# A decoder layer on one core: how the weights of merge, out and FFN are split into two parts

## The reference, cut to what matters

```python
g_a, g_b, g_m = jnp.split(sigmoid(g_raw + b_gate), N_BRANCH, axis=-1)
m = g_a * (o_mla @ w_o_mla) + g_b * (o_ssm @ w_o_ssm) + g_m * (o_mem @ w_o_mem)
x1 = layer_norm(ALPHA * x + m @ w_out, ln1_g, ln1_b)
h = jnp.square(relu(x1 @ w_up + b_up))          # w_up (1024, 4096)
y = layer_norm(ALPHA * x1 + h @ w_down + b_down, ln2_g, ln2_b)
```

## Time and profile before

| what | value |
|---|---|
| runs | 1709.58 us median of 3 (1708.92 to 1711.88) |
| profiled execution, first to last instruction (span) | 1706.6 us |
| around the span, against the median | 3.0 us |
| instructions | 25877 |
| granted TensorE clock, mean | 0.991 |
| busy: TensorE, VectorE, ScalarE, GpSimd | 1662.8, 756.0, 408.1, 404.1 us |
| DMA | 206.23 MB, mean 121 GB/s |
| transfers on SyncE's queue into the ring | 216, 512.0 KB each |
| transfers on GpSimd's queue (pages) | 128, 160.0 KB each |

### The profile page before, as it was taken

One profiled execution on the slowest core, in us unless ns is written; L12 is line 12 of the kernel. 1 busy time (PEld: TensorE's weight loads), 2 busy tenths in 40 slices (PEclk: granted clock), 3 DMA queues, 4 the chain that ended last, 5 costly groups with the idle time before them and its releaser, 6 DMA issues.

```text
span 1706.6 us, 25877 instructions
## 1 busy us (share of the span) xinstructions
PE 1662.8 (97%) x10438; PEld 1408.6 (83%) x10438; DVE 756.0 (44%) x1312; ACT 408.1 (24%) x800; POOL 404.1 (24%) x344
## 2 busy tenths in 40 slices
PE   8999999999999999999999999999997999999995
PEld 6877787787877777787777777789997999999995
DVE  5667687774431111112122122344478760177334
ACT  2252433425211211111111110142224111111122
POOL 0041231314020000000333300113435444444332
PEclk9999999999999999999999999999998999999998
DMA  5424233352361221223787765332221222222221
GB/s 179 163 81 164 79 125 123 95 180 81 124 214 62 64 73 62 63 76 112 237 252 236 235 250 197 138 129 93 87 87 51 87 87 87 87 87 87 87 62 53
DMA packets 70409, 206.23 MB, mean 121 GB/s; under 512 B 10161, under 2 KB 26802, under 8 KB 65682
## 3 DMA queue, kind: packets, MB, share of 16 engines
q1 hardware_dynamic: 50384, 151.67, 27.4%
q10 hardware_dynamic: 13762, 31.93, 5.4%
q0 software_dynamic: 6144, 20.98, 4.0%
HBM read 189.68 MB, written 14.86 MB: 120 GB/s over the span
## 4 chain that ended last, share of the span: by engine, by line
PE 90%; DVE 5%; issue 1%; ACT 1%; DMA 1%; POOLq 0%; POOL 0%; SPq 0%; DVEq 0%; ACTq 0%
PE acc L1734 31%; PE acc L1774 29%; PE acc L2076 7%; PE acc L2043 3%; PE acc L2026 2%; PE acc L2179 1%; PE bank L2091 1%; PE bank L2110 1%; PE bank L2092 1%; DVE work L1217 1%; PE bank L2193 1%; PE bank L2061 1%; PE bank L2067 1%; PE bank L2131 1%; PE bank L2264 1%
## 5 line engine op out<-in xcount | busy, mean ns | idle before, releaser
L1734 PE MATMUL acc<-xt,ring 128*128 128x272 f32 x2272 | 543.2, 395 | 0.0
L1734 PEld LDWEIGHTS acc<-xt,ring 128*128 128x128 f32 x2272 | 425.8, 190 | 101.1 <-issue 17.6
L1774 PE MATMUL acc<-x_parts,f_parts 128*128 128x272 f32 x1408 | 220.9, 293 | 11.9 <-DVE x_parts L1144 10.7
L522 POOL TENSOR_TENSOR f_parts<-ring,f_parts 128x1024 fp32r<-128x1024 f32 x65 | 157.7, 2426 | 247.8 <-ACT f_parts L701 247.6
L1774 PEld LDWEIGHTS acc<-x_parts,f_parts 128*128 128x128 f32 x1408 | 197.4, 192 | 14.5 <-issue 8.0
L500 POOL DMA_DIRECT2D work<-in_page_cols x128 | 69.0, 539 | 464.1 <-PE bank L2131 354.3
L1774 PE MATMUL acc<-f_parts 128*128 128x272 f32 x1344 | 172.2, 289 | 0.0
L1774 PEld LDWEIGHTS acc<-f_parts 128*128 128x128 f32 x1344 | 170.4, 188 | 0.1
L701 ACT ACTIVATE f_parts<-ring 128x1024 fp32r<-128x1024 f32 x65 | 69.0, 1061 | 238.6 <-PE acc L1774 204.2
L2076 PE MATMUL acc<-branch,ring 128*128 128x272 f32 x512 | 120.0, 392 | 0.0
L2076 PEld LDWEIGHTS acc<-branch,ring 128*128 128x128 f32 x512 | 96.0, 190 | 18.8
(11 more groups left out here) (351 smaller groups left out, 2042.0 us busy)
## 6 DMA issues: line engine op xcount, KB each, us to landing
ring<-in_stream SPq DMA_DIRECT2D x216, 512.0 KB, 3.6
work<-in_page_cols POOLq DMA_DIRECT2D x128, 160.0 KB, 3.2
attended<-in_ssm_state ACTq DMA_DIRECT2D x8, 1024.0 KB, 6.2
work<-cum_rows SPq DMA_DIRECT2D x32, 256.0 KB, 4.5
out_ssm_s<-attended ACTq DMA_DIRECT2D x8, 1024.0 KB, 5.6
work<-in_ckv_rows ACTq DMA_DIRECT2D x64, 128.0 KB, 3.6
work<-in_ckv_rows SPq DMA_DIRECT2D x64, 128.0 KB, 3.0
work<-in_memk_cols SPq DMA_DIRECT2D x8, 1024.0 KB, 6.6
```

The costliest lines, as they stand in the source:

```text
L522: pool.tensor_tensor(lo, ring[:, s * BLOCK:(s + 1) * BLOCK], hi.bitcast(F), SUB).then_inc(sem["split_ready"], 1)
L1734: m = pe.matmul(acc[p][:, half, 0:width], w[:, k * P:(k + 1) * P], x(kk)[:, half * width:(half + 1) * width], start=kk == 0, stop=kk == n_ ...
L1774: m = pe.matmul(acc_half, w[:, k * P:(k + 1) * P], x[:, kk, of], start=kk == 0 and n == 0, stop=kk == last and n == 2)
```

## The change

GpSimd no longer subtracts, and SyncE no longer loads, from block `SPLIT_FROM` on. Each of the 86 blocks is now split by two transfers on GpSimd's queue and one operation of ScalarE. `round_block` issues a transfer from the stream, float32, into `w_high`, whose type is float32r, so that the transfer converts. ScalarE's `negate` writes the negative of this into `w_low`. `rest_of_block` issues a second transfer of the same block from the stream, which adds onto `w_low` (`accum_op=ADD`), so that it holds w - wh. `w_high` has four slots and takes the place of the ring in memory; `w_low` has four slots in `f_parts`. The three pairs of buffers are gone.

`round_block(i)` waits until TensorE has begun the block three before it; `rest_of_block(i)` waits for the landing of the one before it and for ScalarE's negation of block i. TensorE waits for `w_rest` before each block. GpSimd issues for each block first the rounding transfer, then the adding one, then goes on to the next block. Before the first layer norm 25 blocks are issued in full (24 before); the rounding transfer of the next goes out between the two halves of `X_L`, its adding transfer behind them. In the merge, ScalarE negates blocks 2j and 2j+1 before it reads gate j. Two semaphores of another stage are merged into one (`latent_summed`).

```diff
-        ring = sb("ring", RING * BLOCK)
+        with ExitStack() as whole_weights:
+            ring = whole_weights.enter_context(nc.sbuf_tensor("ring", [P, RING * BLOCK], F))
+        w_high = sb("w_high", RING * BLOCK, R)
...
-        split = [[k(BLOCK) for _ in range(2)] for _ in range(2)]
...
+        w_low = [k(BLOCK) for _ in range(RING)]
 
         def split_of(i):
...
+            s = (SPLIT_FROM + i) % RING
+            return w_high[:, s * BLOCK:(s + 1) * BLOCK], w_low[s]
...
+            def round_block(i):
+
+                at = SPLIT_FROM + i
+                hi, _ = split_of(i)
+                if i < RING - 1:
+                    pool.wait_ge(sem["blocks_begun"], CREDIT["blocks_begun"] + at - RING + 2)
+                else:
+                    pool.wait_ge(sem["split_begun"], CREDIT["split_begun"] + i - RING + 2)
+                pool.dma_start(hi, stream[at]).then_inc(sem["w_rounded"], 16)
+
+            def rest_of_block(i):
+
+                _, lo = split_of(i)
+                if i:
+                    pool.wait_ge(sem["w_rest"], t.next("w_rest", 16))
+                pool.wait_ge(sem["negated"], t.next("negated"))
+                pool.dma_start(lo, stream[SPLIT_FROM + i], accum_op=ADD).then_inc(sem["w_rest"], 16)
+
             def split_block(i):
-
-                s, (hi, lo) = (SPLIT_FROM + i) % RING, split_of(i)
-                pool.wait_ge(sem["hi_ready"], t.next("hi_ready"))
-                pool.tensor_tensor(lo, ring[:, s * BLOCK:(s + 1) * BLOCK], hi.bitcast(F),
-                        SUB).then_inc(sem["split_ready"], 1)
-                pool.wait_ge(sem["split_ready"], t.next("split_ready"))
-            pool.wait_ge(sem["mem_used"], 2 * DEC_BATCH)
+                round_block(i)
+                rest_of_block(i)
             t.skip("rounded", 2 * KC)
-            for i in range(MERGE_SPLIT + N_SPLIT[0] + 2):
+            for i in range(MERGE_SPLIT + N_SPLIT[0] + 3):
                 split_block(i)
...
-                    if h == 0 and c == 3:
-                        split_block(MERGE_SPLIT + N_SPLIT[0] + 2)
-            for i in range(MERGE_SPLIT + N_SPLIT[0] + 3, MERGE_SPLIT + sum(N_SPLIT)):
+                if h == 0:
+                    round_block(MERGE_SPLIT + N_SPLIT[0] + 3)
+            rest_of_block(MERGE_SPLIT + N_SPLIT[0] + 3)
+            for i in range(MERGE_SPLIT + N_SPLIT[0] + 4, MERGE_SPLIT + sum(N_SPLIT)):
                 split_block(i)
...
-            load(sum(n * b for _, n, b in PHASES) - blocks_before("merge_m") - 2)
+            assert block_at.value() == SPLIT_FROM
...
-            def split_block(i):
-
-                s, (hi, _) = (SPLIT_FROM + i) % RING, split_of(i)
...
-                act.activation(hi, ring[:, s * BLOCK:(s + 1) * BLOCK], ACT.Copy).then_inc(sem["hi_ready"], 1)
-                act.wait_ge(sem["hi_ready"], t.next("hi_ready"))
+            def negate(i):
+
+                hi, lo = split_of(i)
+                act.wait_ge(sem["w_rounded"], t.next("w_rounded", 16))
+                act.activation(lo, hi.bitcast(F), ACT.Copy, scale=-1.0).then_inc(sem["negated"], 1)
...
             for j in range(1, KC):
+                negate(2 * j)
+                negate(2 * j + 1)
                 read_gate(2, j)
-                split_block(2 * j)
-                if j < KC - 1:
-                    split_block(2 * j + 1)
...
+            def next_split():
+
+                pe.wait_ge(sem["w_rest"], t.next("w_rest", 16))
+                return split_of(splits.next() - 1)
```

More of the change, by code:

```diff
@@ L155 @@
               "st_p_stored", "var_ready", "std_ready",
-              "squares_ready", "cq_summed", "ckv_summed", "kr_folded", "krope_ready",
+              "squares_ready", "latent_summed", "kr_folded", "krope_ready",
               "latents_ready", "new_turned", "new_read", "act_over", "head_read", "q_lat_ready", "q_lat_read", "k_ready",
@@ L169 @@
 SEMAPHORES += ["q_b_ready", "sums_ready", "norm_summed",
-               "centred", "partly_summed", "shift_read", "half_ready", "recentred", "low_even", "low_odd", "squared", "rounded", "hidden_ready", "hi_ready", "split_ready", "split_begun", "scaled", "biased"]
+               "centred", "partly_summed", "shift_read", "half_ready", "recentred", "low_even", "low_odd", "squared", "rounded", "hidden_ready", "w_rounded", "w_rest", "negated", "split_begun", "scaled", "biased"]
 def program(nc, stream, x_t, mem_t, const, vec, conv_state, ssm_state, pages, ckv_rows, page_cols,
@@ L555, in load @@
                     s = at % RING
[L556 to L560, removed]
+                    if at >= RING:
                         sp.wait_ge(sem["blocks_begun"], CREDIT["blocks_begun"] + at - RING + 2)
@@ L988, in _ @@
                 act.activation(X0_H[:, c, :], X[:, c, :], ACT.Copy).then_inc(sem["rounded"], 1)
-            for s in range(RING):
-                t.skip(f"weights_in_slot{s}", 16 * loaded_before(SPLIT_FROM, s))
-            split_block(0)
+            negate(0)
             read_gate(2, 0)
@@ L997, in _ @@
             t.skip("rounded", 2 * KC)
-            split_block(1)
+            negate(1)
             act.wait_ge(sem["acc1_ready"], t.value("acc1_ready"))
@@ L1010, in _ @@
             act.activation(act_mark[0:1, 1:2], act_mark[0:1, 0:1], ACT.Sqrt)
-            for i in range(1, 6):
-                split_block(MERGE_SPLIT + i)
+            for i in range(2, 6):
+                negate(MERGE_SPLIT + i)
             squares(out_sq, *((c, whole) for c in range(3)))
-            split_block(MERGE_SPLIT + 6)
+            negate(MERGE_SPLIT + 6)
             for c in range(3, KC - 1):
                 squares(out_sq, (c, whole))
-                if c < 6:
-                    split_block(MERGE_SPLIT + c + 4)
+                negate(MERGE_SPLIT + c + 4)
             squares(out_sq, (7, halves[0]), (7, halves[1]))
             std()
-            split_block(MERGE_SPLIT + 10)
             gain_bias("ln1g", "ln1b", [(c, of) for of in halves for c in range(KC)], True)
             last = MERGE_SPLIT + sum(N_SPLIT) - 2 * KC
-            for i in range(MERGE_SPLIT + N_SPLIT[0] + 3, last + 8):
-                split_block(i)
+            for i in range(MERGE_SPLIT + N_SPLIT[0] + 3, last + 9):
+                negate(i)
             squares(down_sq, *((c, whole) for c in range(3)))
             for c in range(3, KC - 1):
[L1028 to L1032, removed]
+                for i in range(2 * c + 3, min(2 * c + 5, 2 * KC)):
+                    negate(last + i)
+                squares(down_sq, (c, whole))
+            squares(down_sq, (7, halves[0]), (7, halves[1]))
             std()
@@ L1454, in variance @@
                 m.then_inc(sem[signal], 1)
-            variance(a_rstd, lambda half: bank[half], "cq_summed", Q_LORA, "var_ready")
+            variance(a_rstd, lambda half: bank[half], "latent_summed", Q_LORA, "var_ready")
             group_var()
-            variance(k_rstd, lambda half: acc[0][:, half, :], "ckv_summed", KV_LORA, "var_ready")
+            variance(k_rstd, lambda half: acc[0][:, half, :], "latent_summed", KV_LORA, "var_ready")
             t.skip("var_ready", 2)
@@ L1783, in project_parts @@
                 for b in range(n_blocks):
-                    wh, wl = split_of(splits.next() - 1)
-                    pe.wait_ge(sem["split_ready"], t.next("split_ready"))
+                    wh, wl = next_split()
                     for half, of in enumerate(halves):
@@ L1800, in project_last_chunk_last @@
             def project_last_chunk_last(xh, xl):
-                pair = [split_of(splits.next() - 1) for _ in range(2)]
+                pair = []
                 for p in range(2):
                     pe.wait_ge(sem[f"acc{p}_free"], t.next(f"acc{p}_free"))
-                    pe.wait_ge(sem["split_ready"], t.next("split_ready"))
+                    pair.append(next_split())
                     for half, of in enumerate(halves):
@@ L2006, in _ @@
             pe.wait_ge(sem["pair_read"], t.next("pair_read", 2))
-            rms(a_sq[0:3], lambda half: bank[half], "cq_summed")
+            rms(a_sq[0:3], lambda half: bank[half], "latent_summed")
             group_sums()
@@ L2015, in _ @@
             pe.wait_ge(sem["squares_ready"], t.next("squares_ready", 2))
-            rms(a_sq[3:5], lambda half: acc[0][:, half, :], "ckv_summed")
+            rms(a_sq[3:5], lambda half: acc[0][:, half, :], "latent_summed")
             pe.wait_ge(sem["mem_loaded"], 16)
```

## The result

The changed kernel takes 1913.68 us (median of 3 runs, 1912.59 to 1913.97) against 1709.58 before: a ratio of 1.1183, 95% interval [1.1167, 1.1198], 204 us slower. The forecast was 1870, in a range of 1707 to 2080; the loop and the direction were right, the loss was forecast at 160 us and is 204.

What follows compares the result with a forecast made beforehand. TensorE, busy 97%, was taken as the bound. 79 blocks losing 2.0 us each gave 159 us on the 1706.6 us span, 1866; plus 3.0 to the median, 1869, rounded to 1870 us, range 1707 to 2080.

Steps and rivals of the forecast that it cites:

- the loop: GpSimd's queue, per block: adding transfer issued, next rounding issued and landed, ScalarE negates, GpSimd wakes; slower than TensorE's 6.04 us.
- the appetite of 6.04 us: Up projection: TensorE takes 6.04 us for one block of 48 matmuls, the pace the split must meet.
- Its period: One turn of GpSimd's loop: 3.4 landing, 3.45 occupation by the adding transfer, 1.2 negation and wake; 8.05 us.
- adding transfer's occupation D: Time the adding transfer occupies the 16 DMA engines: 2 x 1.73 = 3.45 us, bounded by 1.73 and 5.2.
- The number of blocks: Blocks losing 2.0 us each: 19 of 22 up to the norm, 60 behind it; 79, 159 us.
- during the norm ... the pair's two blocks are there: First layer norm: TensorE's 18 us away exceed two loop turns, so the pair's two blocks are ready.
- the lead of three blocks: Start of the split: the first three of 22 blocks come early and lose nothing.
- The signs it named: Down stretches: TensorE idle about 2 us per block, starts 8 us apart, DMA share near 0.65, adding landing near 5.5 us.
- A: Rival: the loop fits under 6.04 us, period 4.9 to 6.1; not slower, 1707 to 1710 us; chance 0.19.
- B: Rival: adding or converting much dearer than its bytes, period 9.8 us or more, 2007 us; clock may fall; chance 0.18.
- C: Rival: VectorE holds up GpSimd's descriptor writing in the up halves, 50 us more, 1920 us; chance 0.05.
- D: Rival: both transfers move like plain ones, nothing added on the way, occupation 1.73 us; 1730 us; chance 0.06.

Runs made afterwards that it cites:

- e1: Changed kernel with GpSimd issuing the rounding transfer of block i+1 ahead of the adding transfer of block i: 1709.82 us, 0.9998 of the kernel before.
- e2: As e1, and an adding transfer waits only for the last but one: 1709.32 us, 0.9991 of the kernel before.
- e5: e2 with block 25 split inside the first layer norm, and block 26's rounding first behind it: 1707.24 us, 0.9985 of the kernel before.
- e3: Changed kernel with ScalarE's negation of each block done twice: 2011.03 us, 1.1753 of the kernel before.
- e4: Changed kernel whose second transfer overwrites w_low, converting, and adds nothing (lower weight parts wrong): 1770.77 us, 1.0349 of the kernel before.
- e6: Changed kernel in its own issue order, but an adding transfer waits only for the last but one: 1910.44 us, 1.117 of the kernel before.
- e7: Changed kernel with negations 23 and 24 and block 24's adding transfer moved later around the first layer norm: 1904.62 us, 1.1137 of the kernel before.

## Why the prediction was right, and where it was off

**What bounded the kernel, and the appetite of 6.04 us**: right. e1, e2 and e5 are at TensorE's pace again.

**The loop and its place**: right, shown from four sides: taken apart (e1: all 204 us back), lengthened (e3: 97 us), shortened (e4: 143 us), and a wait outside it removed (e6: no change clear of noise).

**Its period**: forecast 8.05 us, measured 8.46 and 8.58. The terms:

| term | forecast | measured |
|---|---|---|
| issue lag | 0.54 to 1.15 | 0.55 |
| rounding with nothing ahead of it, to landing | 3.4 | 3.9 |
| adding transfer's occupation D | 3.45 | 3.10 |
| rounding as queued, to landing | 6.3 | 6.2 median |
| negation | 1.06 | 1.07 |
| GpSimd from the negation to its issue | 0.14 | 0.53 or more |

The occupations are the share of the 16 engines times the length of a window with one transfer alone: plain in the kernel before, then converting, then adding in the changed one (queue: packets, MB, share of 16 engines; transfer: median us to landing).

```profile
q1 hardware_dynamic: 144, 0.52, 27.9%
```

```profile
q0 software_dynamic: 144, 0.52, 31.3%
...
w_high<-in_stream POOLq DMA_DIRECT2D x1, 512.0 KB, 3.9
```

```profile
q0 software_dynamic: 144, 0.52, 43.1%
...
f_parts<-in_stream POOLq DMA_DIRECT2D x1, 512.0 KB, 5.5
```

27.9% of 5.5 us is 1.53 us for the plain one, 31.3% of 5.6 is 1.75 for the converting one, 43.1% of 7.2 is 3.10 for the adding one. So the choice of two passes for the addition fits: 3.10 is 2.0 times the plain 1.53, and 1.8 times the converting 1.75. The Trainium skill, "Collectives: The Full Stack", section "Stop ④ — SDMA + CCE: where bytes move and the add happens", describes the addition in a collective's transfer as read, read, write; this trace agrees, with 3.10 us against 1.53. What was taken too high was the plain 1.73: 8.59 MB are 16.4 blocks and not 16, which gives 1.68, and the rest is the difference between a stretch and one transfer alone. What was too low was the landing; the two cancel. Over the whole run, the rounding transfers (L522) land after 3.9 to 7.5 us, 6.2 in the median, and the adding ones (L530) after 5.0 to 7.0, 5.5 in the median.

What made the forecast of the period too short is the last term. 0.14 us was the wake for an arithmetic instruction; a DMA on GpSimd's queue starts 0.5 us or more behind the semaphore ("issue" in the chain). 0.4 us on 82 turns is 33 us, an estimate, of the 45 us by which the forecast was short. How much less than D the queueing costs was also off: e4 takes 1.35 us of occupation away and the landing falls by 1.7, and e4's own 4.5 us is only 0.6 over the 3.9 alone where D minus lag says 1.2. I can't say which part of the transfers overlaps.

**The number of blocks**: this step failed in its first part. The sum of spans: block 0 begins 1.6 us later than before (1140.68 against 1139.05; 1139.03 in e2 and 1139.28 in e6, so this is no price of the change); from there to the pair behind the norm it takes 202.1 us instead of 146.4, 55.7 more; from there to the end 146.9 more; 204.3 in all. Behind the norm the forecast was 60 blocks, and 59 x (8.58 - 6.04) = 150 fits. Ahead of it the forecast was 19 blocks, and the loss is that of 55.7 / 2.42 = 23. The chain says which: it runs in the loop from the negation of block 1 to that of block 24, 23 turns, and leaves it there for the norm's square (L681) and the sum behind it:

```profile
1137.81 1.05 ACT f_parts L703
...
1332.19 1.06 ACT f_parts L703
1333.25 0.33 ACT work L681
...
1333.62 0.74 PE bank L1769 x2
```

So both ends were misjudged. At the far end, the step "during the norm ... the pair's two blocks are there" took the norm as time that hides the loop. In truth the norm's squares are queued on ScalarE behind the negations, so the norm waited for the loop. In e7, with another order of ScalarE and GpSimd around the norm, block 0 to the pair takes 195.2 us: 7.0 of the 55.7 are back, and 48.7 / 2.42 = 20 blocks are left. At the near end, the lead of three blocks shrank: only round(0) was early, since round(1) stands behind rest(0) and this behind the negation at 1129.57. Blocks 0 and 1 still came in time. By the landing of its adding transfer (issued at 1147.79, 5.5 us) block 2 would have come about 0.2 us late; TensorE waited 3.19 us for it, because the gate that it needs first stands behind the negation of block 3:

```profile
1156.29 0.52 PE L1774 MATMUL acc<-f_parts,w_high 128*128 128x272 f32 x2 [3.19 <-ACT work L907]
```

The 3 us that the forecast added for the merge are of this kind, and they are paid only with the loop: e1 and e2 have the same order of ScalarE, and take 145.5 us from block 0 to the pair.

**What the miss is made of**: the longer turn, 0.41 us on 23 turns and 0.53 on 59, is 41 us; three turns more at 2.0 us are 6. Together that is 47 of the 45 us missed, so the size of the turn was the larger error and the number of blocks the smaller.

**The signs it named.** TensorE's idleness before a block is 1.5 us on average and not 2, although the turn is longer: at a granted clock of 0.90 its own work takes longer and fills part of the gap. The DMA share is 0.55 and not 0.65, with D at 3.10. The adding transfer lands in 5.5 us as stated. For the converting one "near 5" was a slip: the sum itself has it at 6.3 as queued, and it measured 6.2.

**What it gives back**: forecast 1.7 to 3.0 us from a quieter VectorE. The slow case of L1126 is gone (the same line, L1122 in e2, takes 0.45 us at 1289.53 where it took 2.15), and e5's span is 2.1 us under that of before. VectorE's L1697, 2511 ns beside GpSimd's subtraction, takes 443 ns in the changed kernel (L1692 there); in the chain before it stands once, at 1308.91.

**Rivals.** A (it fits under 6.04) is refuted for the change as made, and is what e1 makes true. B: the addition was not dearer than two passes over its bytes. The clock did fall, to 0.90, at the edge of the 0.5 to 0.9 that B named, and TensorE is busy 75 us longer for the same 10438 matmuls. But this time lies in its waits for the loop: the chain runs through the transfers, GpSimd waited for TensorE once, and e1 has both the time and the clock back without any change to TensorE's work. C (VectorE holds up GpSimd's descriptors): no sign. Between the starts of L522, a turn takes 8.46 us in the first up projection (1363.50 to 1473.45, 13 turns) and 8.50 in the second (1629.17 to 1748.10, 14), with VectorE busy 35 and 30% of the time; it takes 8.50 in the first down projection (1483.16 to 1619.09, 16) and 8.70 in the second (1756.43 to 1869.46, 13), with VectorE at 7.5 and 15%. The rule of the Trainium skill, "SBUF — State Buffer", in its box on VectorE blocking DMA, is neither shown nor refuted by this: the turns beside more work of VectorE aren't longer than the others. D is e4 in part: 1770, not 1730.

## What to carry to other kernels

Where an engine issues dependent transfers in program order, write down its loop: everything between one issue and the same issue of the next block, with the landing as it is when queued behind its own predecessor, and compare it with the consumer's pace before anything else. One block of look-ahead in the order of issue was worth 204 us here, with not a byte less moved. And a pause of the bottleneck hides such a loop only if the work of the pause isn't queued behind the loop on some engine (7 us here, e7).

## What was not expected of the hardware

A converting transfer of 512 KB on GpSimd's queue occupies the 16 DMA engines only 1.75 us against 1.53 plain and lands in 3.9 us with nothing ahead of it (3.5 at least in e1 and e4); one that adds, 3.10 us and 5.5. TensorE at 100% at 2.4 GHz goes along with a DMA share of 0.82, practically all of it on GpSimd's queue (e1: 81.4% of the engines between 1400 and 1500 us). GpSimd's DMA instruction shows 0.54 us alone and 0.86 when it adds or follows an adding one, but the next starts 0.52 us behind a converting one (e4) and 0.55 behind an adding one.
